# One program instead of three in a hybrid decoder step, values stationary, and the softmax divided before its transposes

## The chip, the cores and the metric

The kernel runs on one core of a Trainium2 chip. The metric is the device time of one execution in microseconds (us). Names of engines: TensorE (PE, its weight loads PEld), VectorE (DVE), ScalarE (ACT), GpSimd (POOL), and SyncE (SP), which here issues every DMA.

## The reference, cut to what matters

One layer of a decoder over 2048 prompt tokens and 32 sample tokens (8 sequences of 4 steps), model width 1024, everything in float32:

```
proj = x @ w_in                        # 22 column tiles of 128 and 8 gate columns
A: mLSTM, 4 heads of 128, chunkwise: scores, decay, a state C (128x128) and n per head
B: attention in a window of 128, 8 query heads on 2 key heads of 64, with a sink per head:
   mx = max(max(s), snk);  p = exp(s - mx)
   p / (sum(p) + exp(snk - mx))        # then @ v
x = LayerNorm(alpha * x + concat(A, B) @ w_out)
x = LayerNorm(alpha * x + (silu(x @ w1) * (x @ w3)) @ w2)
```

Outputs are both token groups' activations, the states, and the last 128 keys and values.

## The kernel before, in words

**Products.** Tokens are split into five groups of 416 columns (`TG`). A matrix is taken in slabs of 8 tiles of 128x128 (512 KB). To keep float32 accuracy, ScalarE rounds a slab to `whi`, GpSimd takes the rest `wlo = raw - whi`, and TensorE makes three products per tile, hi*hi, hi*lo and lo*hi, so a slab is 24 matmuls of 416 columns (`product`, L258). x is split in the same way, in quarters (`round_x`, `split_x`) when a visit of a token group begins. `raw` and `wlo` have four buffers, `whi` three: the load of slab n+3 waits for slab n-1, its rounding for slab n.

**Three programs.** `mixers` runs slabs 0 to 133 (110 of the projection, then those of the output product), `tail` slabs 134 to 149, `layer` the five groups' FFN, 60 slabs each. Each is a Block of its own, so all engines meet at its end.

**The order.** Every engine walks the same slabs n; tables written out by hand say after which slab what is done. `BASES` gives the slab at which a chunk of 128 tokens begins, `PIECES` its six pieces: TURN (transposes of k and v, first window scores, mLSTM scores), MIX (transposes of the first two exponentials, mLSTM outputs, state products), WIN (other window scores, first values), TURN2 (transposes of the other exponentials), VALUES (other values, transposes of the mLSTM output), OUT (`turn_out`: transposes of the attention's output `ow`). Most chunks have the offsets (0, 2, 3, 5, 6, 7), five have (0, 1, 2, 3, 4, 5). `LOAD_X_AT` and `SPLIT_AT` place the loads and splits of x, `ROWS_AT` the loads of a chunk's gate rows, broadcast over the partitions, `GATES_AT` the gate tables' chain.

**The attention in a chunk.** `window_max` adds the bias to the scores and takes the maximum; `window_exp` on ScalarE writes the exponentials to `pw` and their sums to `psums`; `turn_window` transposes them; `copy_turned` copies them to `ptw`. `window_values` has `ptw` stationary and 64 columns of v moving: 16 matmuls a chunk. In `valued`, VectorE divides by sums and sink into `ow`, four transposes turn it, and ScalarE copies it to `mix`.

**The tail.** The samples' inputs are loaded at slab 134 (`load_sample`), their scores, heads, transposes and outputs follow after slabs 135 to 138. Their mix goes to DRAM, and the last visit of the output product (slab 142 on) reads it with the prompt's part. The first LayerNorm of the first group stands at slabs 138 to 142 (`NORM`), eight state updates at 143 to 146 (`UPDATES`), the first FFN slabs' loads and rounding at 143 and after.

**The layer.** While a group's FFN runs, two LayerNorms are under way, one step per slab: SUM 0, MEAN 1, CENTRE 2, SQUARE 3, SUM_SQ 4, VARIANCE and ROOT 5, SCALE 6. The last group's second LayerNorm stands at the end, alone.

Of the kernel before, what the change touches and what calls it, by code (L numbers as in the profile page):

```python
# [48 lines left out]
X_AT = LIMIT - 2 * KD * TG * 4  # L49
assert AHEAD_AT % 32 == 0  # L50
# [20 lines left out]
class Store:  # L71


    def __init__(self, nc, ctx, at, end=LIMIT):
        self.nc, self.ctx, self.at, self.end = nc, ctx, at, end
# [9 lines left out]

    def ps(self, name, shape):
        return self.ctx.enter_context(self.nc.psum_tensor(name, shape, F32))
# [5 lines left out]
def load_gates(sp, io, t):  # L93
# [5 lines left out]
    for i, (n, bias) in enumerate((("gi", "b_ig"), ("gf", "b_fg"))):  # L99
# [18 lines left out]
CUT = PROJ + 3 * KD  # L118
# [9 lines left out]
LOAD_X_AT = (None, None, 3, 6, 9, 22, 44, 66, 88, 110, 118, 126, 141)  # L128
SPLIT_AT = (None, (0, 0, 1, 1), (3, 4, 4, 4), (6, 7, 7, 7), (9, 10, 10, 10), (26, 27, 32, 33), (47, 48, 54, 55), (69, 70, 76, 77),
            (97, 98, 103, 104), (112, 113, 115, 116), (120, 121, 123, 124), (128, 129, 131, 132), (141, 141, 141, 141))  # L130
# [3 lines left out]
PIECES = tuple(tuple(b + o for o in (FIVE if c in (1, 9, 10, 11, 14) else SEVEN)) for c, b in enumerate(BASES))  # L134
# [4 lines left out]
ROWS_AT = (21,) + tuple(b + 1 for b in BASES[:-1])  # L139
# [38 lines left out]
class Stream:  # L178


    def __init__(self, nc, ctx, io, m):
# [3 lines left out]
        self.raw = Store(nc, ctx, m.at).sb("raw", [P, 4, KD, P])  # L185
# [3 lines left out]
        for b, a in enumerate((Store(nc, ctx, X_AT), m)):  # L189
            self.xh.append(a.sb(f"xh{b}", [P, KD, TG], F32R))  # L190
            self.xraw.append(Store(nc, ctx, a.at).sb(f"xraw{b}", [P, KD, TG]))
            self.xl.append(a.sb(f"xl{b}", [P, KD, TG], F32R))
        self.ring_at = m.at

        self.stage = [Store(nc, ctx, m.at + (i * RING + FREE) * 4).sb(f"stage{i}", [P, TG]) for i in range(STAGES)]
# [15 lines left out]
    def load_x(self, sp, v, q):  # L211

        last = {2: gate_tile(1), 3: gate_tile(2), 4: gate_tile(3)}.get(v)
        if 5 <= v <= MIXED + 1:
            last = slab_tile((v - 4) * NPROJ - 1)
        if v > MIXED + 1:
            last = slab_tile(PROJ + (v - MIXED - 1) * KD - 1)
        if last is not None:
            sp.wait_ge(self.acc_full, last + 1)
        ks, (g, b) = slice(q * XQ, q * XQ + XQ), VISITS[v]  # L220
        src = self.io["xT"][g, :, ks] if v < MIXED else self.io["mixT"][ks, :, g * TG:g * TG + TG].rearrange("t p n -> p t n")
        sp.dma_start(self.xraw[b][:, ks], src).then_inc(self.x_in[v % 2][q], 16)
# [69 lines left out]
def mixers(nc, io, ctx, keep, outs, s_inp, stream):  # L292
# [5 lines left out]
    with ExitStack() as ctx:  # L298
        m = Store(nc, ctx, x.ring_at, X_AT)
        ring = m.sb("ring", [P, NPROJ, RING])  # L300

        xs = m.sb("xs_b", [P, H, 2, C])
        bias = m.sb("bias", [P, 8, SPAN])
        state, nlast, mix, mix_out, kv_out, st_out = (outs[n] for n in ("state", "nlast", "mix", "mix_out", "kv_out", "st_out"))
        causal = m.sb("causal", [P, C])
        ones = m.sb("ones", [P, 1])
        sinks = m.sb("sinks", [P, 8])
        gml = m.sb("gml", [P, H])
        vaug = m.sb("vaug", [P, H, P + 1])
        vs = m.sb("vs", [P, 2, P])  # L310
        pw = m.sb("pw", [P, 2, 2, SPAN])
        shared = m.at

        t = Store(nc, ctx, shared, X_AT)
        g = {n: t.sb(n, s) for n, s in (
            ("gi", [R, C]), ("gf", [R, C]), ("gi_s", [H, NS]), ("gf_s", [H, NS]),
            ("small", [R, 4]), ("small_s", [H, 4]), ("m0_sb", [H, DB]))}
        g["loaded"] = t.sem("g_loaded")
        gi, gf, gis, gfs, small, small_s, m0, g_loaded = (
            g[n] for n in ("gi", "gf", "gi_s", "gf_s", "small", "small_s", "m0_sb", "loaded"))  # L320
        tile = lambda n: (t.sb(n, [R, C]), t.sb(n + "_s", [H, NS]))
        b, b_s = tile("b")
        run, runs = tile("run")
        u, us = tile("u")
        em, ems = tile("em")
        own = t.sb("own", [R, C])
        gx, gxs = t.sb("xs", [R, 2, C]), t.sb("xss", [H, 2, NS])
        ones_r = t.sb("ones_r", [R, C])
        m_last = t.sb("m_last", [H, DB])
        m_end = t.sb("m_end", [1, H])  # L330
        ends = t.sb("ends", [1, 2, H, NC])
        after = t.sb("after", [1, H, NC])
        before = t.sb("before", [1, H, NC])
        inherited = t.sb("inherited", [R, 1])

        early = Store(nc, ctx, x.ring_at + EARLY * RING * 4, x.ring_at + NPROJ * RING * 4)
        anti = early.sb("anti", [P, P])
        hank = early.sb("hank", [P, 8, SPAN])
        srow = early.sb("srow", [32, 132])
        repl = early.sb("repl", [32, P])  # L340
        srow_all = early.sb("srow_all", [P, 132])
        smask = early.sb("smask", [P, 2, NS])
        onehot = early.sb("onehot", [32, HJ])
        relb = early.sb("relb", [32, 8])
        outside = early.sb("outside", [8, HJ])
        ext = early.sb("ext", [8, HJ])
        graw = early.sb("graw", [P, KD, 8])
        ghi = early.sb("ghi", [P, KD, P], F32R)
        glo = early.sb("glo", [P, KD, P], F32R)
        grow = early.sb("grow", [8, 2, TG])  # L350

        w = Store(nc, ctx, shared, X_AT)
        decay = w.sb("decay", [P, H, C])
        qs = w.sb("qs", [P, H, C])

        hn = Store(nc, ctx, w.at).sb("hn", [P, H, P])
        prob = w.sb("prob", [P, H, C])
        ow = Store(nc, ctx, w.at).sb("ow", [P, 4, P])
        kw = w.sb("kw", [P, H, P])
        den = w.sb("den", [P, H])  # L360
        ucol = w.sb("ucol", [P, 2, 2, H])
        rec = w.sb("rec", [P, H])
        ssq = w.sb("ssq", [P, H])
        root = w.sb("root", [P, H])
        gate = w.sb("gate", [P, H, C])
        sq8 = w.sb("sq8", [P, J, C])
        nmx = w.sb("nmx", [P, 8])
        mx = w.sb("mx", [P, 8])
        psums = w.sb("psums", [P, 2, 8])
        snk = w.sb("snk", [P, 8])  # L370
        ptw = w.sb("ptw", [P, 2, 4, W])

        acc = [m.ps(f"acc{i}", [P, 512]) for i in range(2)]
        w01 = m.ps("w01", [P, 2, 512])
        ce = m.ps("ce", [P, 2, 512])
        kd, fb = m.ps("kd", [P, 512]), m.ps("fb", [P, 512])
        heads_out = ce[:, :, 0:258].rearrange("p b (h e) -> p b h e", e=P + 1)
# [31 lines left out]
        def place(c):  # L409
            return slice(c * C % RING, c * C % RING + C)  # L410
# [1486 lines left out]
```

## Time and profile before

| | us |
|---|---|
| median of 3 runs (lowest, highest) | 2575.45 (2573.36, 2578.94) |
| the profiled execution | 2576.87 |
| its span, first to last instruction | 2575.1 |
| TensorE busy | 2493.3 |
| GpSimd busy | 1287.1 |
| ScalarE busy | 937.3 |
| VectorE busy | 927.6 |

The profile is of one execution. Its span begins with the first instruction, and all times in the rows below count from there; the execution took 1.8 us more than the span.

### The profile page before, as it was taken

The numbers are of one execution on the slowest core, as the hardware profiler recorded it, in microseconds if no ns is written. First come the engines' busy times: TensorE is split into PE (matmuls) and PEld (weight loads), VectorE is DVE, ScalarE is ACT, GpSimd is POOL, SyncE is SP. The second block draws the span as 40 slices with busy tenths as digits, with TensorE's granted clock in tenths as the row PEclk, the third lists the DMA queues.
The fourth block names the chain that finished last, engine by engine and source line by source line (L and its number), as shares of the span: only waits on it lengthen the run. The fifth ranks groups of instructions, "written<-read, shape, count | busy, mean of one in ns | idle before, by whom it ended". The sixth has DMA issues, their size and how long they took to land.

```text
span 2575.1 us, 33629 instructions
## 1 busy us (share of the span) xinstructions
PE 2493.3 (97%) x13771; PEld 2427.3 (94%) x13771; DVE 927.6 (36%) x1535; ACT 937.3 (36%) x1415; POOL 1287.1 (50%) x544
## 2 busy tenths in 40 slices
PE   8989999999999988999999999999999999999997
PEld 7979999999999877899999999999999999999996
DVE  4345454444546444111424213421335114251104
ACT  3324444444455423222334224332244223342222
POOL 4444544445444434455545565555554555555552
PEclk9999999999999988999999999999999999999998
DMA  5443534434365663434334343344333443334331
GB/s 185 152 118 97 143 99 136 105 99 142 97 183 177 200 216 116 128 119 143 124 106 135 119 155 113 105 136 146 125 114 99 144 145 122 108 120 132 124 117 68
DMA packets 142480, 335.50 MB, mean 130 GB/s; under 512 B 14734, under 2 KB 79846, under 8 KB 141670
## 3 DMA queue, kind: packets, MB, share of 16 engines
q1 hardware_dynamic: 142326, 333.34, 41.4%
q8 instruction: 110, 1.80, 0.3%
q14 instruction: 44, 0.36, 0.0%
HBM read 305.05 MB, written 29.26 MB: 130 GB/s over the span
## 4 chain that ended last, share of the span: by engine, by line
PE 57%; DVE 2%; ACT 0%; issue 0%; ACTq 0%; DVEq 0%
PE l_acc L1670 19%; PE l_acc L1668 19%; PE l_acc L1669 19%; DVE l_total L1128 1%; DVE hl L1704 0%; PE var L1144 0%; PE mean L1140 0%; ACT nxt L1651 0%; DVE nxt L1763 0%; DVE part L1718 0%; DVE var L1765 0%; DVE hbuf L1700 0%; DVE nxt L1713 0%; ACT x_squares L1646 0%; DVE hh L1702 0%; DVE l_total L1718 0%
## 5 line engine op out<-in xcount | busy, mean ns | idle before, releaser
L1605 POOL TENSOR_TENSOR l_wlo<-l_raw,l_whi 128x1024 fp32r<-128x1024 f32 (+1 forms) x297 | 823.7, 2773 | 693.6 <-ACT l_whi L1614 693.6
L1614 ACT ACTIVATE l_whi<-l_raw 128x1024 fp32r<-128x1024 f32 (+1 forms) x297 | 340.8, 1148 | 1031.2 <-PE l_acc L1670 992.8
L253 POOL TENSOR_TENSOR wlo<-raw,whi 128x1024 fp32r<-128x1024 f32 x150 | 364.7, 2432 | 543.0 <-ACT whi L247 542.8
L1668 PE MATMUL l_acc<-xh,l_whi 128*128 128x416 f32 x1760 | 620.0, 352 | 7.9 <-PEq L1190 7.9
L1670 PE MATMUL l_acc<-xh,l_wlo 128*128 128x416 f32 x1760 | 621.9, 353 | 0.0
L1669 PE MATMUL l_acc<-xl,l_whi 128*128 128x416 f32 x1760 | 615.1, 350 | 0.0
L266 PE MATMUL acc<-xh,whi 128*128 128x416 f32 x1072 | 385.4, 359 | 0.0
L268 PE MATMUL acc<-xh,wlo 128*128 128x416 f32 x1072 | 378.1, 353 | 0.0
L267 PE MATMUL acc<-xl,whi 128*128 128x416 f32 x1072 | 375.5, 350 | 0.0
L1668 PEld LDWEIGHTS l_acc<-xh,l_whi 128*128 128x128 f32 x1760 | 331.0, 188 | 11.3 <-issue 8.8
L1669 PEld LDWEIGHTS l_acc<-xl,l_whi 128*128 128x128 f32 x1760 | 331.2, 188 | 6.7 <-issue 1.3
L1670 PEld LDWEIGHTS l_acc<-xh,l_wlo 128*128 128x128 f32 x1760 | 330.6, 188 | 2.0
L1700 DVE TENSOR_TENSOR hbuf<-silu,l_acc 128x416 f32<-128x416 f32 x110 | 64.6, 588 | 732.7 <-PE l_acc L1670 732.7
L247 ACT ACTIVATE whi<-raw 128x1024 fp32r<-128x1024 f32 x150 | 158.4, 1056 | 466.5 <-PE acc L268 269.4
L1668 PE MATMUL l_acc<-hh,l_whi 128*128 128x416 f32 x880 | 312.1, 355 | 0.0
L1669 PE MATMUL l_acc<-hl,l_whi 128*128 128x416 f32 x880 | 309.4, 352 | 0.0
L1670 PE MATMUL l_acc<-hh,l_wlo 128*128 128x416 f32 x880 | 308.6, 351 | 0.0
L267 PEld LDWEIGHTS acc<-xl,whi 128*128 128x128 f32 x1072 | 202.2, 189 | 2.4
L268 PEld LDWEIGHTS acc<-xh,wlo 128*128 128x128 f32 x1072 | 201.6, 188 | 2.3
L266 PEld LDWEIGHTS acc<-xh,whi 128*128 128x128 f32 x1072 | 202.2, 189 | 1.4 <-POOL wlo L253 0.3
L1668 PEld LDWEIGHTS l_acc<-hh,l_whi 128*128 128x128 f32 x880 | 167.0, 190 | 2.5 <-issue 1.4
L1670 PEld LDWEIGHTS l_acc<-hh,l_wlo 128*128 128x128 f32 x880 | 165.2, 188 | 1.7
(333 smaller groups left out, 2567.6 us busy)
## 6 DMA issues: line engine op xcount, KB each, us to landing
l_raw<-in_wB SPq DMA_DIRECT2D x220, 512.0 KB, 3.6
raw<-in_wA SPq DMA_DIRECT2D x110, 512.0 KB, 3.7
l_raw<-in_w SPq DMA_DIRECT2D x80, 704.0 KB, 4.0
raw<-in_wB SPq DMA_DIRECT2D x40, 512.0 KB, 4.1
xraw<-in_xT SPq DMA_DIRECT2D x32, 416.0 KB, 5.6
xraw<-mixT SPq DMA_DIRECT2D x20, 416.0 KB, 6.5
stage<-in_xT SPq DMA_DIRECT2D x40, 208.0 KB, 4.2
pre<-stage SPq DMA_DIRECT2D x40, 208.0 KB, 4.1
```

Of the source, the lines that this page charges most:

```text
L247: self.nc.scalar.activation(self.whi[:, n % 3], self.raw[:, n % 4], ACT.Copy).then_inc(self.hi_done, 1)
L253: self.nc.gpsimd.tensor_tensor(self.wlo[:, n % 4], self.raw[:, n % 4], self.whi[:, n % 3].bitcast(F32), ALU.subtract).then_inc(self.lo_don ...
L266: pe.matmul(bank[:, 0:TG], hi[:, a], self.xh[x][:, a], start=(a == 0), stop=False)
L267: pe.matmul(bank[:, 0:TG], hi[:, a], self.xl[x][:, a], start=False, stop=False)
L268: last = pe.matmul(bank[:, 0:TG], lo[:, a], self.xh[x][:, a], start=False, stop=(a == KD - 1))
L1128: self.nc.vector.tensor_reduce(self.total[:], self.over_tiles(sq), AX.X, ALU.add).then_inc(self.sq_summed, 1)
L1605: nc.gpsimd.tensor_tensor(wlo[:, n % 4, 0:k], raw[:, n % 4, 0:k], whi[:, n % 3, 0:k].bitcast(F32), ALU.subtract).then_inc(S["lo_done"], 1)
L1614: nc.scalar.activation(whi[:, n % 3, 0:k], raw[:, n % 4, 0:k], ACT.Copy).then_inc(S["hi_done"], 1)
L1668: pe.matmul(bank, whi[:, n % 3, c], hx[:, a], start=(a == 0), stop=False)
L1669: pe.matmul(bank, whi[:, n % 3, c], lx[:, a], start=False, stop=False)
L1670: last = pe.matmul(bank, wlo[:, n % 4, c], hx[:, a], start=False, stop=(a == total - 1))
L1700: nc.vector.tensor_tensor(hbuf[:], silu[:, j % 2], acc[:, t % BANKS, 0:TG], ALU.mult).then_inc(S["evac"], 2)
```

## The change

All three parts become functions of one Block. The banks of the accumulators are shared by name, and where the end of a Block kept memory apart, counters are awaited (`Chunks.done`, `ring_read`, `updated`).

In a chunk, ScalarE scales the exponentials by one over (sum and sink's exponential) before they are transposed, per head (`divide`); v is stationary and `ptw` moves, 256 columns at a time, so that the result has the mix's layout. `turn_out`, `ow` and its multiplication are gone.

The samples' inputs are loaded from slab 130, and their mix is written straight into the last visit's x. Slab tables are changed.

```diff
-CUT = PROJ + 3 * KD
+CUT = PROJ + 3 * KD - 1
-LOAD_X_AT = (None, None, 3, 6, 9, 22, 44, 66, 88, 110, 118, 126, 141)
-SPLIT_AT = (None, (0, 0, 1, 1), ..., (26, 27, 32, 33), ..., (141, 141, 141, 141))
-SEVEN, FIVE = (0, 2, 3, 5, 6, 7), (0, 1, 2, 3, 4, 5)
-BASES = (24, 31, 37, 44, 51, 58, 66, 73, 80, 88, 94, 100, 106, 113, 120, 126)
-ROWS_AT = (21,) + tuple(b + 1 for b in BASES[:-1])
+LOAD_X_AT = (None, None, 3, 6, 9, 30, 44, 66, 88, 110, 118, 126, 135)
+SPLIT_AT = (None, (-1, -1, 0, 0), ..., (34, 35, 40, 41), ..., (139, 139, 140, 140))
+BASES = (24, 31, 37, 44, 51, 58, 66, 73, 80, 88, 94, 100, 106, 113, 119, 126)
+PIECES = tuple(tuple(b + o for o in (0, 2, 3, 5, 6, 6)) for b in BASES)
+SAMPLE_AT = BASES[-1] + 4
+ROWS_AT = (22,) + tuple(b + 1 for b in BASES[:-1])
-        GATES_AT = 15
+    GATES_AT = 14
...
@@ sync of the mixers
+        x.load(sp, 3)
             for n in range(CUT):
+            if n:
                 x.load(sp, n + 3)
-                if n == GATES_AT + 5:
+            if n == GATES_AT + 6:
                     sp.wait_ge(ga, SCALES)
+            if n == SAMPLE_AT:
+                chunks.ring_read(sp)
+                load_sample(sp, io, sample)
@@ tensor
-                wait(pe, "p_exp", c, r + 1)
+            wait(pe, "p_normed", c, r + 1)
-            def window_values(c, r):
-                wait(pe, "pt_copied", c, r + 1)
-                for gr in range(2):
-                    for half in range(2):
-                        last = pe.matmul(fb[:, r * P + gr * 64:r * P + gr * 64 + 64], ptw[:, r % 2, 2 * gr + half],
-                                         vs[:, s if half else 1 - s, gr * 64:gr * 64 + 64], ...
+        def window_values(c, pair):
+            wait(pe, "pt_copied", c, 2 * pair + 2)
+            for half in range(2):
+                for gr in range(2):
+                    last = pe.matmul(fb[64 * gr:64 * gr + 64, pair * 2 * W:pair * 2 * W + 2 * W], vs[:, s if half else 1 - s, gr * 64:gr * 64 + 64],
+                                     ptw[:, :, 2 * gr + half], start=(half == 0), stop=(half == 1))
-            def turn_out(c):
-                wait(pe, "ow_ready", c)
-                for r in range(J):
-                    last = pe.transpose(ce[:, 1, r * C:r * C + C], ow[:, r], ident[:])
-                last.then_inc(S["o_turned"], 1)
@@ scalar
+        def sink_exp(c, pair):
+            wait(act, "snk_arg", c, pair + 1)
+            a = slice(4 * pair, 4 * pair + 4)
+            nc.scalar.activation(snk[:, a], snk[:, a], ACT.Exp).then_inc(S["snk_exp"], 1)
+        def divide(c, pair):
+            wait(act, "rs_ready", c, pair + 1)
+            for r in (2 * pair, 2 * pair + 1):
+                for gr in range(2):
+                    last = nc.scalar.activation(pw[:, r % 2, gr], pw[:, r % 2, gr], ACT.Identity, scale=snk[:, 2 * r + gr:2 * r + gr + 1])
+                last.then_inc(S["p_normed"], 1)
@@ vector: sums after the exponentials, no ow
+        def sums(v, c, pair):
+            wait(dve, "snk_exp", c, pair + 1)
+            wait(dve, "p_exp", c, 2 * pair + 2)
+            v(nc.vector.tensor_tensor(snk[:, a], snk[:, a], psums[:, s, a], ALU.add))
+            nc.vector.reciprocal(snk[:, a], snk[:, a]).then_inc(S["rs_ready"], 1)
@@ tail
-    FIRST, SCORES, HEADS, TURNED, OUT, NORM, UPDATES = (CUT + i for i in (0, 1, 2, 3, 4, 4, 9))
+    FIRST, SCORES, HEADS, TURNED, OUT, UPDATES = (CUT + i for i in (0, 1, 2, 3, 4, 6))
+    HIGH_AT, FFN_AT = LAST + 2, LAST + 2
+    mix = x.xraw[VISITS[-1][1]][:, :, SEQ - (NG - 1) * TG:TG]
+    norm_at = {"sum": CUT + 1, "mean": CUT + 2, "centre": CUT + 3, "square": CUT + 4, "sum_sq": CUT + 5, "variance": CUT + 7, "scale": CUT + 8, "gain": CUT + 9}
-                if n == OUT + 1:
-                    sp.wait_ge(sig["mixed"], 3)
-                    sp.dma_start(io["mixT"][:, :, SEQ:NT].rearrange("t p n -> p t n"), mix[:]).then_inc(S["mix_out"], 16)
+            if n == LOAD_X_AT[-1]:
                     sp.wait_ge(outs["mix_out"], 16 * NC)
-                    sp.wait_ge(S["mix_out"], 16)
@@ layer
-    SUM, MEAN, CENTRE, SQUARE, SUM_SQ, VARIANCE, ROOT, SCALE, GAIN, HIGH, LOW = 0, 1, 2, 3, 4, 5, 5, 6, 7, 9, 10
+    SUM, MEAN, CENTRE, SQUARE, SUM_SQ, VARIANCE, ROOT, SCALE, GAIN, HIGH, LOW = 0, 1, 2, 3, 4, 6, 6, 7, 8, 10, 11
@@ layer, the last LayerNorm: four adds for two reduces, ScalarE squares and copies the mean, GpSimd centres tiles 4 to 7
+        for k in range(4, KD):
+            nc.gpsimd.tensor_tensor(x[:, k], x[:, k], silu[:, 1], ALU.subtract).then_inc(centred_rest, 1)
-            sum_part(part, 0, 0, 4)
-            sum_part(norm.total, 1, 4, 7)
+        add_squares(x_squares[:, 0:2], slice(0, 2), slice(2, 4), 1)
+        add_squares(part[:], 0, 1, 2)
+        add_squares(x_squares[:, 4], 4, 5, 3)
+        add_squares(norm.total[:], 4, 6, 4)
```

## Rows read from the trace of the kernel before

**Rows 1.** The page: busy time of each engine.
```profile
PE 2493.3 (97%) x13771; PEld 2427.3 (94%) x13771; DVE 927.6 (36%) x1535; ACT 937.3 (36%) x1415; POOL 1287.1 (50%) x544
```

**Rows 2.** Stretches of TensorE: length, busy (instructions), granted clock, DMA share, GB/s.
```profile
161.09:176.99 15.90, 6.54 (x31) 0.68 0.48 184
886.33:897.12 10.79, 6.64 (x23) 0.68 0.64 174
904.48:914.28 9.80, 5.20 (x45) 0.65 1.11 374
935.50:948.37 12.87, 12.87 (x53) 0.60 0.36 99
959.65:979.04 19.39, 5.72 (x15) 0.56 0.18 56
992.79:1003.07 10.28, 7.45 (x28) 0.67 0.33 96
1028.05:1040.54 12.49, 4.62 (x14) 0.73 0.61 188
886.33:1036.27 149.94, 116.82 (x619) 0.83 0.55 174
1200.00:1250.00 50.00, 50.00 (x266) 1.00 0.39 126
```

**Rows 3.** TensorE's waits: waiter, releaser, us in total, times, longest.
```profile
PE var L1144 <- DVE l_total L1128: 5.3, 4, 1.3
...
PE w L590 <- ACT pw L719: 3.0, 3, 1.3
...
PE acc L266 <- DVE ring L869: 2.2, 1, 2.2
```

**Rows 4.** Timeline of TensorE in chunk 2's WIN: start, us, instruction.
```profile
278.54 1.14 PE L577 MATMUL w<-ring,sq 64*128 64x256 f32 x8
279.61 2.00 PE L599 MATMUL fb<-vs,ptw 128*128 128x64 f32 x16
281.42 0.44 PE L266 MATMUL acc<-xh,whi 128*128 128x416 f32 x1
```

**Rows 5.** Timeline of TensorE: bias tables (512 columns), samples' window scores.
```profile
54.06 1.98 PE L677 MATMUL w<-hank,anti 128*128 128x512 f32 x4
55.88 1.88 PE L677 MATMUL ce<-hank,anti 128*128 128x512 f32 x4
...
909.43 0.68 PE L1326 MATMUL s_wi<-s_kc,s_qb 128*32 128x128 f32 x8 [4.60 <-DMA s_state<-in_state_C]
...
909.98 0.67 PE L1326 MATMUL s_wi<-s_kc,s_qb 128*32 128x128 f32 x8
```

**Rows 6.** Timeline of chunk 12: ScalarE's last exponential, then TensorE's MIX.
```profile
715.88 0.50 ACT L719 ACTIVATE pw<-pw,nmx 128x256 f32<-128x256 f32 x1
716.28 0.19 ACT L719 ACTIVATION_READ_ACCUMULATOR pw<-pw,nmx 128x1 f32 x1
...
719.15 0.60 PE L590 MATMUL w<-ident,pw 128*128 128x128 f32 x4
```

**Rows 7.** Timeline of SP's issues, before chunk 0 and in the tail.
```profile
146.68 1.13 SPq L489 DMA_DIRECT2D xsT<-xs  x2
...
151.23 7.22 SPq L222 DMA_DIRECT2D xraw<-in_xT  x4
...
897.63 6.31 SPq L1094 DMA_DIRECT2D s_state<-in_state_C  x4
```

**Rows 8.** Timeline of VectorE in the tail.
```profile
943.72 6.06 DVE L1120 TENSOR_REDUCE t_total<-nxt 128x416 f32<-128x3328 f32 x1
...
974.27 3.82 DVE L280 TENSOR_TENSOR xl<-xraw,xh 128x832 fp32r<-128x832 f32 x4
```

**Rows 9.** The chain that ended last, its end: start, us, what.
```profile
2550.39 3.19 DVE part L1718
2553.59 1.50 DVE l_total L1718
...
2560.71 3.59 DVE nxt L1763 x2
```

More of the change, by code:

```diff
@@ new lines, in mixers @@
+    m = Store(nc, x.ring_at, X_AT)
+    ring = m.sb("ring", [P, NPROJ, RING])
+    xs = m.sb("xs_b", [P, H, 2, C])
+    bias = m.sb("bias", [P, 8, SPAN])
+    state, nlast, mix, mix_out, kv_out, st_out = (outs[n] for n in ("state", "nlast", "mix", "mix_out", "kv_out", "st_out"))
+    causal = m.sb("causal", [P, C])
+    ones = m.sb("ones", [P, 1])
+    sinks = m.sb("sinks", [P, 8])
+    gml = m.sb("gml", [P, H])
+    vaug = m.sb("vaug", [P, H, P + 1])
+    vs = m.sb("vs", [P, 2, P])
+    pw = m.sb("pw", [P, 2, 2, SPAN])
@@ new lines, in mixers @@
+    shared = m.at
+    t = Store(nc, shared, X_AT)
+    g = {n: t.sb(n, s) for n, s in (
+        ("gi", [R, C]), ("gf", [R, C]), ("gi_s", [H, NS]), ("gf_s", [H, NS]),
+        ("small", [R, 4]), ("small_s", [H, 4]), ("m0_sb", [H, DB]))}
+    g["loaded"] = t.sem("g_loaded")
+    gi, gf, gis, gfs, small, small_s, m0, g_loaded = (
+        g[n] for n in ("gi", "gf", "gi_s", "gf_s", "small", "small_s", "m0_sb", "loaded"))
+    tile = lambda n: (t.sb(n, [R, C]), t.sb(n + "_s", [H, NS]))
+    b, b_s = tile("b")
@@ new lines, in mixers @@
+    run, runs = tile("run")
+    u, us = tile("u")
+    em, ems = tile("em")
+    own = t.sb("own", [R, C])
+    gx, gxs = t.sb("xs", [R, 2, C]), t.sb("xss", [H, 2, NS])
+    ones_r = t.sb("ones_r", [R, C])
+    m_last = t.sb("m_last", [H, DB])
+    m_end = t.sb("m_end", [1, H])
+    ends = t.sb("ends", [1, 2, H, NC])
+    after = t.sb("after", [1, H, NC])
+    before = t.sb("before", [1, H, NC])
+    inherited = t.sb("inherited", [R, 1])
+    early = Store(nc, x.ring_at + EARLY * RING * 4, x.ring_at + NPROJ * RING * 4)
@@ L1179, in layer_inputs, with tail @@
     }
[L1182 removed]
+def tail(nc, io, keep, s_inp, outs, stream, chunks, taken, ahead, norm, ps):
     cols, ident, sbias = keep["cols"], keep["ident"], keep["sbias"]
@@ L1519, in layer @@
-def layer(nc, io, keep, stream, ahead):
+    LAST = PROJ + 4 * KD - 1
+    FIRST, SCORES, HEADS, TURNED, OUT, UPDATES = (CUT + i for i in (0, 1, 2, 3, 4, 6))
+    HIGH_AT, FFN_AT = LAST + 2, LAST + 2
+    m = taken["rest"]
+    inp, (xs, state, n0, kc, vc, causal, sinkcol, gml) = s_inp, (
+        taken[n] for n in ("xs", "state", "n0", "kc", "vc", "causal", "sinkcol", "gml"))
+    expo = m.sb("s_expo", [NS, H, NS])
+    decay = m.sb("s_decay", [NS, H, NS])
+    prob = m.sb("s_prob", [NS, H, NS])
```

2460 lines of the change are left out of this document (1225 added, 1235 removed).

## The prediction, made before the changed kernel ran

> **What bounds the kernel now.** I read the page first. TensorE is busy 97% of the span [rows 1], so a microsecond is won only by giving it less to do, by closing its gaps, or by not letting its clock fall. Second, the stretches: in an undisturbed one the granted clock is 1.00 and 266 products of 416 columns start in 50 us, 0.188 us each [rows 2]. With that price any other stretch can be audited: its length less the work in it is what was lost. Third, the waits of TensorE [rows 3] and the order of time in one chunk say whose fault a loss is.
>
> The audit. From 886.33, where the first program's last piece begins, to 1036.27, where the layer begins, are 149.9 us [rows 2]. The work is 16 slabs of 24 products (72.2 us) and the samples' pieces (I add their pieces in the timeline to 28.3 us): 100.5 us. So 49 us are lost, one by one [rows 2]: 10.8 us for 0.4 + 3.5 of work at the first program's end (6.9 lost); 9.8 us for 3.3 of work before the samples' scores (6.5); 19.4 us for 2.8 before the last visit (16.6); 10.3 for 5.7 at the first state updates (4.6); 12.5 for 2.6 at the second program's end (9.9); and some 4 at half clock around the samples' last matmuls. Each loss has two parts: the gap, and a restart in which the clock stands at 0.5 for some us: the mean clock of these stretches is 0.56 to 0.73. Elsewhere: 15.9 us at chunk 0 for 8 products and its TURN, 4.0 of work (11.9 lost) [rows 2]; 2.2 us on a ring copy in the fourth slab; 3.0 us on the exponentials in three chunks that have one slab between TURN and MIX; and four waits at the variance, 5.3 us in all [rows 3].
>
> **The change, part by part.**
>
> *Values stationary.* Now each chunk makes 16 matmuls of 64 columns on full arrays, in two passes each: the 16 records from 279.61 to the next slab at 281.42 are 0.11 us each [rows 4]: 1.73 us and the way back to full slabs. VALUES holds the other 16 and four transposes of 0.09. New: 8 matmuls of 256 columns, 16 passes, each half writing 64 of the 128 output partitions. The nearest rows for 256 columns are the scores: 8 passes from 278.54 to 279.61, 1.07 us [rows 4]. At half the price of 512 columns (4 records from 54.06 to 55.88, 0.455 us each [rows 5]) they would take 0.23 each and 1.8 us one after another, so the two row halves run side by side. I read the 1.07 us as four steps of 0.215 and 0.2 for two changes of the array's shape. Column parts of the array run side by side too: the samples' scores write 32 partitions each, and the first 8 records of 128 columns, with 8 of 32 behind them, are through in 0.55 us (909.43 to 909.98 [rows 5]), where one after another at half clock the 8 alone would take over 1.7. I therefore take 4 x 0.215 = 0.86 for each half chunk instead of 1.73, and 0.1 for each of three more changes of the array's shape. WIN: 2.87 becomes 2.03; VALUES: 2.09 becomes 1.42; the four transposes of `turn_out` (0.36) go. That is 1.87 a chunk, 29.9 us in 16. Bounds: passes one after another give 16 x 0.215 = 3.44 against 3.46, so the part is worth only 5.8 - 4.8 = 1 us; no cost for the shape changes gives 34.7.
>
> The Trainium skill (TensorEngine Tiling, "Key Properties") has the rule that speaks against this: changing the tiling mode drains the engine, while tiles of one mode run independently. The trace agrees with both halves, at about 0.1 us a change. If a drain cost twice that, the sum would be 4.8 us worse.
>
> *The division moves to ScalarE.* Eight scalings of 128x256 a chunk. The exponentials of that shape start 0.41 us apart without the accumulator read [rows 6], so 3.3 us a chunk on an engine that is busy 36% [rows 1]. What hides it is the distance between TURN and MIX, now always two slabs. In the latest chunk (12) the second exponentials end at 716.37 [rows 6]; the sink's exponential and two small VectorE operations add 0.7, four scalings 1.7: 718.8, and MIX starts at 719.15. Margin 0.3 us; chunk 11 is as close, chunk 14, held up by a split on VectorE, may wait, and the rest have 0.7 to 2 by the same reading. The next slab's rounding moves from 716.9 to 719, with its rest on GpSimd 2.4 us later still, two slabs ahead of need. On VectorE the `sums` stand before the value copy, `prob` and `kw`, all needed only at MIX. Cost on the path: 2 us in all. The 3.0 us of waits in one-slab chunks go.
>
> *Gate tables and the load queue.* The 9.4 us gap before chunk 0 is SP's: it stood until 146.68 for the tables, then queued rows and four x loads of 416 KB before the slabs [rows 7]. The tables now run one slab earlier, rows one later, the x load eight later: all 11.9 us go. The wait of 1.9 us for the samples' chain before the tables' transposes keeps its distance and stays. In the start, two splits precede the loop and slab 3's load no longer stands behind the bias table: 2.2 us go [rows 3].
>
> *One program.* The barriers go. The chunks' counters are awaited after slab 133; the last piece is in slab 132, so nothing is late: 6.9 us. At the other end the first FFN slabs are rounded earlier, nothing waits: 9.9 us.
>
> *Samples' inputs.* Eleven loads are issued at slab 130 instead of 134; TensorE's gap and its restart, 6.5 us [rows 2], go. But SP stood 6.3 us at the last four alone before [rows 7], some 12 at all eleven, and the slab load behind them is now as late as that: issue, 4 us landing, rounding and rest end about when slab 134 is due. I charge 2 us.
>
> *The last visit.* Before, its four quarters were loaded only after the samples' mix had gone through DRAM, and their splits stood behind mean, variance and scaling on VectorE: a reduce of 6.1 us, one like it, and then the splits at 974.27 [rows 8]. Now the prompt's part is loaded at 135, the samples' part is written in place, and sum, centre and squares come earlier. By my placing of VectorE's work the splits end some 5 us before slab 142: 16.6 us go. The updates move to slabs 139 to 142 between splits and scaling (3.6 + 2.7 us on VectorE), where update b waits for b-2: I expect three waits of 1 to 3 us, 4 of the 4.6 us remain in another place. Gain 0.6.
>
> *Variance one slab later.* VectorE's 6.2 us reduce no longer ends after TensorE's slab: four times (1.3 gap + 0.5 slow restart), 7.2 us.
>
> *The end.* The sums of squares, 3.19 + 1.50 us [rows 9], become four adds of 2.9 together; they end 1.8 us earlier, at the last slab's end. ScalarE reads the mean while TensorE makes the last variance product, level with the two VectorE operations it replaces. Half of the centring (1.8 of 3.59 us [rows 9]) leaves the chain for GpSimd, which has 3 us to spare before the fifth tile is due; the root with its table load (2 us) fits under the other half. I take 3.5 us.
>
> **Sum.** 29.9 - 2 + 3.0 + 11.9 + 2.2 + 6.9 + 9.9 + 6.5 - 2 + 16.6 + 0.6 + 7.2 + 3.5 = 94.2 us. The profiled execution took 2576.9 us (span 2575.1): 2482.7. The median of the three runs is 1.4 lower: 2481 us.
>
> **Rivals.**
> - *Passes of the two column halves run one after another* (chance 0.10). For: they read the same partitions of the moving tile in two streams of 256 columns, which no row shows at full clock. Against: [rows 5]. 29 us less gained: 2510.
> - *The tail keeps a stall* (0.16): SP's late slab load, or VectorE late with splits or updates so that slab 142 waits, each with a restart at half clock as in [rows 2]. For: reduces of 6 us in an engine with strict order, margins of a few us. Against: each of these operations has a slab or more between its due time and its need by my placing. 16 of the 38.5 us won there would be given back, three such restarts: 2497.
> - *MIX waits for the division* (0.10): margin 0.3 us in chunk 12. If sums or scalings take 1.5 us more than I say, all chunks wait, 16 x 1.3 = 20 us: 2501.
> - *The clock falls in the new pieces* (0.02), the one that ends slower. The samples' matmuls on narrow parts of the array begin at 935.5 at full clock, and yet the stretch to 948.37 has a mean of 0.60, with TensorE busy all of it [rows 2]. If both column-tiled pieces of each chunk did that, 32 times, it decides from 94/32 = 2.9 us each; that stretch lost about 5, which would give 2576 + 66 = 2642. Against: the new pieces last 0.86 us, not 7.5, with wide streams, and the row-tiled scores beside them run at a clock of 1.00.
> - *More than forecast* (0.05): updates and slab 134 without a wait, no restart after the samples: about 2470.
> - The forecast, 0.57; its own range is 2470 to 2492.
>
> The range reaches to the second and third rival and leaves out the first and fourth (0.12): 2466 to 2504. A difference under 0.2%, 5 us, can't be told from none here. Only the clock rival is slower, and equality would need several rivals at once: faster 0.97, same 0.01, slower 0.02.
>
> **What would show it.** In the profile after: 8 fb matmuls a chunk whose records come in pairs about 0.2 us apart (else the first rival); WIN near 2.0 us; a clock of 1.00 in every stretch from 200 to 850; no wait of TensorE on `pw`; no gap before chunk 0; no gap on PEq at the two former boundaries; the way from slab 133's end to the layer near 108 us instead of 150; no wait at `var`. Wrong it would be if TensorE waited in new places for `pw`, `xl`, `s_state` or `wlo`.

## The result and the profile after

The changed kernel takes 2489.06 us (median of 4 runs, 2486.23 to 2490.38), the kernel before beside it 2577.19 (4 runs, 2573.36 to 2581.67). The ratio is 0.9656 with a 95% interval of 0.9637 to 0.9675: 88.1 us faster. The forecast was 2481, 94 us won, with a range of 2470 to 2492 of its own and of 2466 to 2504 with the rivals. The profiled span went from 2575.1 to 2486.4, so 88.7 us can be followed in the two traces.

The page after (compare [rows 1]): ScalarE has 54 us more work, TensorE 46 us less, and TensorE is still the bound.
```profile
PE 2447.4 (98%) x13451; PEld 2366.3 (95%) x13451; DVE 912.0 (37%) x1566; ACT 991.3 (40%) x1561; POOL 1304.0 (52%) x548
```

TensorE's waits after (compare [rows 3]). Nothing waits for `pw`, nothing in the layer for the variance, and no gap is put down to TensorE's own queue. The first two lines are new: `ptw` are the turned exponentials, copied by ScalarE, and `hn` the normalized heads of the mLSTM, made by VectorE; TensorE had waited for neither in the kernel before.
```profile
PE fb L620 <- ACT ptw L751: 6.8, 1, 6.8
PE kd L672 <- DVE hn L977: 5.8, 8, 2.5
...
PE ce L1331 <- DVE s_state L1542: 2.7, 2, 1.4
```

Stretches of TensorE after, with the columns of [rows 2] and the other engines' busy time between: chunk 0 from the tables on; all chunks from 200 us to the last MIX; chunk 15's second transposes and values with slab 133; from slab 133's end to the layer.
```profile
149.00:170.46 21.46, 21.46 (x127) 20.84 (x126) 9.30 (x22) 10.40 (x24) 11.77 (x6) 1.00 0.55 121
200.00:810.44 610.44, 607.21 (x3694) 565.33 (x3693) 306.64 (x849) 360.01 (x827) 303.06 (x154) 1.00 0.48 139
...
835.20:853.34 18.14, 8.83 (x39) 7.09 (x38) 7.47 (x8) 5.14 (x7) 6.97 (x7) 0.72 0.55 165
853.34:961.26 107.92, 105.25 (x615) 98.42 (x614) 62.13 (x100) 38.13 (x50) 53.13 (x25) 0.95 0.59 193
```
The way to the layer is 107.9 us where it was 149.9. But the stretch before it, 18.14 us with 8.83 of work at a mean clock of 0.72, is a new hole.

I cut the span at landmarks that both traces have and set the gain of each part beside the terms of the prediction:

| part | forecast | measured |
|---|---|---|
| start to the bias tables (53.64, now 49.72) | 2.2 | 3.9 |
| from there to MIX of chunk 0 (185.31, now 170.46) | 11.9 | 10.9 |
| to MIX of chunk 15 (853.94, now 810.44) | 15 x 1.87 + 3.0 - 2 = 29.05 | 28.65 |
| to slab 133's end and on to the layer (1036.27, now 961.26) | 38.5 + 1.87 = 40.4 | 31.5: 42.0 won behind slab 133, 10.5 lost before it |
| to the last mean (2545.83, now 2462.56) | 7.2 | 8.3 |
| the end | 3.5 | 5.4 |
| sum | 94.25 | 88.7 |

Five of six parts lie within 2 us of their forecast; nearly all that is missing was lost at one place, chunk 15.

**The pieces.** WIN of chunk 12 after (compare [rows 4]):
```profile
692.34 1.14 PE L597 MATMUL w<-ring,sq 64*128 64x256 f32 x8
693.40 1.08 PE L620 MATMUL fb<-ptw,vs 128*64 128x256 f32 x8
694.42 0.46 PE L268 MATMUL acc<-xh,whi 128*128 128x416 f32 x1
```
2.08 us, forecast 2.03, before 2.87. VALUES takes 1.43 (forecast 1.42) where nothing waits. The eight records come in pairs 0.216 us apart, 7 ns within a pair. That they run side by side can be read against matmuls of the same type over the whole array, a few us on in the same trace:
```profile
685.02 0.39 PE L653 MATMUL ce<-vaug,prob 128*128 128x129 f32 x2
685.24 0.39 PE L654 MATMUL ce<-state,qs 128*128 128x129 f32 x2
```
Two records of 129 columns take 0.22 us, so two of 256 would take 0.44 and eight 1.75; here eight are through in 0.87 and some 0.15 for the change of shape. The records don't say which half of the columns they belong to; that the two of a pair belong to different halves is my reading (see experiment 9).

**Chunk 15.** SyncE's issues, then ScalarE, VectorE and TensorE, around 825 to 847 us. In square brackets is the idle time before an instruction and what ended it:
```profile
825.70 6.09 SPq L1132 DMA_DIRECT2D s_state<-in_state_C  x4
831.83 1.66 SPq L209 DMA_DIRECT2D raw<-in_wB  x1
...
839.41 1.06 ACT L249 ACTIVATE whi<-raw 128x1024 fp32r<-128x1024 f32 x1 [8.85 <-DMA raw<-in_wB]
840.38 0.88 ACT L243 ACTIVATE xh<-xraw 128x832 fp32r<-128x832 f32 x1
841.16 1.06 ACT L751 ACTIVATE ptw<-w 128x512 f32<-128x512 f32 x2
...
841.29 2.49 DVE L282 TENSOR_TENSOR xl<-xraw,xh 128x832 fp32r<-128x832 f32 x1 [10.60 <-ACT xh L243]
843.70 0.16 DVE L975 RECIPROCAL root<-root 128x4 f32<-128x4 f32 x1
843.90 2.10 DVE L976 TENSOR_TENSOR rec<-rec,root 128x4 f32<-128x4 f32 x1
...
842.28 1.98 PE L620 MATMUL fb<-ptw,vs 128*64 128x256 f32 x8 [6.79 <-ACT ptw L751]
846.78 1.11 PE L672 MATMUL kd<-ident,hn 128*128 128x128 f32 x4 [2.52 <-DVE hn L977]
```
Read it from the top. SyncE stands 6.1 us at the last four of the samples' loads; only then does it ask for the weights of slab 134. They land at 839.4, and ScalarE, which takes its work in strict order, has stood 8.85 us idle for them. Behind that rounding are queued the rounding of a quarter of x and the copies of chunk 15's turned exponentials, both of them ready long before. TensorE waits 6.8 us for the copy. VectorE waited 10.6 us for the quarter, splits it ahead of the normalized heads, and TensorE waits 2.5 us more. The first products behind it then start 0.35 us apart instead of 0.19, at a granted clock of 0.5.

**The end** (compare [rows 9]), from the chain that ended last: the centring is down from 3.59 us to 1.79 in the chain. Of the sums of squares, 3.19 + 1.50 us before, one add of 1.04 us is left in it.
```profile
2473.83 1.79 DVE nxt L1812
2475.63 2.68 DVE w L1814
```
The eight products of mean and variance in front of it, before and after, with the columns of the stretches above:
```profile
2555.13:2559.95 4.82, 4.75 (x8) 2.10 (x8) 2.08 (x4) 1.83 (x2) 0.00 (x0) 0.65 0.00 0
2470.07:2473.20 3.13, 3.06 (x8) 1.43 (x8) 1.17 (x2) 1.28 (x3) 0.00 (x0) 1.00 0.00 0
```
Before, TensorE had waited 2.1 us for the sums and then made these products at a mean clock of 0.65. Now it waits 0.3 us and makes them at 1.00, in 1.7 us less.

### The profile page after: what moved, and what is told of

Its sections match the earlier page's. It is cut to its first block, busy times and chain, and to the rows that moved or that the text cites. A ratio compares the mean times of both kernels' runs of the same rounds, so it can differ in the third digit from the quotient of the medians.

```text
span 2486.4 us, 33138 instructions
## 1 busy us (share of the span) xinstructions
PE 2447.4 (98%) x13451; PEld 2366.3 (95%) x13451; DVE 912.0 (37%) x1566; ACT 991.3 (40%) x1561; POOL 1304.0 (52%) x548
## 3 DMA queue, kind: packets, MB, share of 16 engines
q8 instruction: 107, 1.75, 0.3%
## 4 chain that ended last, share of the span: by engine, by line
PE 91%; DVE 4%; ACT 3%; issue 1%; DMA 1%; SPq 1%; ACTq 0%; DVEq 0%
PE acc L1719 10%; PE acc L1717 10%; PE acc L1718 10%; PE acc L268 8%; PE acc L270 8%; PE acc L269 8%; PE kd L1719 5%; PE fb L1719 5%; PE kd L1717 5%; PE fb L1717 5%; PE kd L1718 5%; PE fb L1718 5%; DVE xl L282 1%; PE w L610 1%; PE w L597 1%
## 5 line engine op out<-in xcount | busy, mean ns | idle before, releaser
L1717 PE MATMUL acc<-xh,l_whi 128*128 128x416 f32 x880 | 310.9, 353 | 0.0
L1719 PE MATMUL acc<-xh,l_wlo 128*128 128x416 f32 x880 | 310.6, 353 | 0.0
L1718 PE MATMUL acc<-xl,l_whi 128*128 128x416 f32 x880 | 307.2, 349 | 0.0
L1718 PEld LDWEIGHTS acc<-xl,l_whi 128*128 128x128 f32 x880 | 165.3, 188 | 4.0 <-issue 1.3
L1717 PEld LDWEIGHTS acc<-xh,l_whi 128*128 128x128 f32 x880 | 165.2, 188 | 2.2 <-issue 1.3
L1719 PEld LDWEIGHTS acc<-xh,l_wlo 128*128 128x128 f32 x880 | 165.0, 188 | 1.0
L1717 PE MATMUL acc<-hh,l_whi 128*128 128x416 f32 x440 | 156.2, 355 | 0.0
L1719 PE MATMUL fb<-xh,l_wlo 128*128 128x416 f32 x440 | 155.3, 353 | 0.0
L1719 PE MATMUL kd<-xh,l_wlo 128*128 128x416 f32 x440 | 155.3, 353 | 0.0
L1718 PE MATMUL acc<-hl,l_whi 128*128 128x416 f32 x440 | 154.7, 352 | 0.0
```

The lines of the kernel that those rows point to most:

```text
L1717: pe.matmul(bank, whi[:, n % 3, c], hx[:, a], start=(a == 0), stop=False)
L1718: pe.matmul(bank, whi[:, n % 3, c], lx[:, a], start=False, stop=False)
L1719: last = pe.matmul(bank, wlo[:, n % 4, c], hx[:, a], start=False, stop=(a == total - 1))
```

## The experiments

All are edits of the changed kernel. Times are medians; their differences are against its 2489.06.

**1. State loads later** (e1). The five loads of the samples' state leave `load_sample` for a function of their own, which takes the first and last of them to issue.
```diff
             if n == SAMPLE_AT:
                 load_sample(sp, io, sample)
+            if n == SAMPLE_AT + 1:
+                load_state(sp, io, sample, 0, 2)
+            if n == SAMPLE_AT + 2:
+                load_state(sp, io, sample, 2, 4)
...
             if n == CUT:
+                load_state(sp, io, taken, 4, 5)
```


> The five loads of the samples' state leave slab 130 of SyncE's order and go out at slabs 131 (two), 132 (two) and 133 (one). Theory A (the stall in chunk 15 is the load queue's: the weights of slab 134 are asked for behind eleven loads and land late, their rounding waits on ScalarE, and the copy of the turned exponentials and the quarter's rounding stand behind it): TensorE's waits of 6.8 and 2.5 us at VALUES of chunk 15 and the slow restart go, slab 133 ends near 843 us instead of 853.3, and the time is 9 to 10.5 us shorter, about 2479. Rival B (ScalarE is late there by its own work, the eight scalings that the change gave it): the waits stay, 2489. Rival C (the state now lands late for the samples' heads in slab 135): TensorE waits there on the state for some us, and a part of the gain is lost, 2482 to 2486.

Measured: 2478.94 us (2476.91 to 2481.75), ratio to before 0.9619, interval 0.9606 to 0.9633; 10.1 us faster. The wait for `ptw` is gone, of the eight waits for `hn` the longest is 0.8 us, and slab 133 ends at 842.04 instead of 853.34. SyncE asks for the weights of slab 134 at 825.22, where it had asked at 831.83, and their rounding, which had started at 839.41 after 8.85 us of idle time, starts here:
```profile
825.22 0.33 SPq L209 DMA_DIRECT2D raw<-in_wB  x1
...
830.97 1.06 ACT L249 ACTIVATE whi<-raw 128x1024 fp32r<-128x1024 f32 x1 [0.75 <-DMA raw<-in_wB]
```
So 6.6 of the 8.4 us are the later asking. The rest is a slower landing, which took 7.6 us behind the four loads and 5.8 us here.
Theory A held in place and size. The state is not late for the heads.

**2. Order in two engines** (e2). ScalarE copies before it rounds, VectorE normalizes before it splits, in every chunk; the loads are those of the changed kernel.
```diff
-            x.round_slab(act, n + 3)
             for c in at_piece(n, TURN2):
                 copy_turned(c, 2)
                 copy_turned(c, 3)
+            x.round_slab(act, n + 3)
...
             x.add(dve, acc, n)
+            for c in at_piece(n, TURN2):
+                normed(v, c)
             for k in range(1, len(VISITS)):
```


> Loads as in the changed kernel; only the order in two engines is changed, in every chunk: ScalarE copies the turned exponentials before it rounds a slab, VectorE normalizes before it splits a quarter of x. Theory A: the late weights are themselves early enough for slab 134 (they land near 839 us, rounding and rest end near 844, and the slab is due after 845), only what is queued behind their rounding hurt. So the stall goes just as with later loads, 9 us, and the seven waits of 0.46 us on the normalized heads go too, 3 us: about 2477. Rival (the late weights themselves hold TensorE): a wait on the rest of slab 134 of 3 to 8 us takes the place of the old one, 2480 to 2487. Rival B (ScalarE's own work is what is late): no gain but the 3 us, 2486.

Measured: 2485.45 us (2483.55 to 2487.52), 3.6 faster, in a range that overlaps the changed kernel's; the reading rests on the trace. Both waits in chunk 15 go, and another takes their place, which neither theory named:
```profile
843.92 2.66 DVE L282 TENSOR_TENSOR xl<-xraw,xh 128x832 fp32r<-128x832 f32 x1
846.50 0.68 DVE L986 SCALAR_TENSOR_TENSOR mixed<-kd,gate 128x512 f32<-128x512 f32 x1
...
847.28 0.58 PE L1342 MATMUL kd<-ident,s_inp 128*32 128x128 f32 x2 [5.44 <-DVE mixed L986]
```
The quarters' rounding still stands behind the late weights, the splits behind it, and the mix of chunk 15 behind the splits. The samples' transposes (L1342) write the bank that this mix still reads. So a late load that nobody needs yet reached TensorE by a second way. The order decides which waiter is hit; the cure is the load. The waits of 0.46 us for `hn` did not go either (seven, 3.2 us in all): my reading that a split in front causes them was wrong (see the last section).

**3. Three blocks again** (e3).
```diff
+        for sync, gpsimd, tensor, scalar, vector in parts:
+            with nc.Block() as block:
+                block.sync(sync)
+                ...
```


> The changed kernel in three blocks again, with the barrier after slab 132 and the one after the last slab of the first product. By the prediction's two terms it loses 6.9 us at the first and 9.9 us at the second, 16.8 in all: 2506, with gaps of TensorE's queue of 4 to 6 us at both places and a slow restart behind each. Rival: at the first boundary the stall of chunk 15 covers part of it, and the rounding of the first slabs behind the second boundary is done before it, so that only 5 to 10 us are lost: 2494 to 2499.

Measured: 2503.38 us (2502.45 to 2508.14), 14.3 slower. Two gaps on TensorE's queue are back:
```profile
PE kd L1717 <- PEq L1857: 7.9, 1, 7.9
...
PE acc L268 <- PEq L1857: 3.8, 1, 3.8
```
From slab 133's end to the layer it takes 117.6 us (856.21 to 973.84) against 107.9: 9.7 for the second barrier, forecast 9.9. From the second transposes of chunk 15 to slab 133's end it takes 28.2 us against 23.4: 4.8 for the first, forecast 6.9. The stall of chunk 15 is in both.

**4. Window values twice** (e4).
```diff
-            for half in range(2):
+            for half in (0, 1, 0, 1):
                 for gr in range(2):
                     last = pe.matmul(fb[64 * gr:64 * gr + 64, ...
```


> The eight matmuls of 256 columns that make a chunk's window values are issued twice, into the same place, so the output stays. If the two halves of the array's columns run side by side, four of them add 0.87 us, and 32 groups add 28 us: 2517. If their passes run one after another, four take 1.7 to 1.8 us and 32 groups add 56 us: 2545. If the clock fell in them, more than that, with a granted clock under 0.98 in the chunks.

Measured: 2509.91 us (2507.88 to 2510.70), 20.9 slower, with a granted clock of 0.993, as in the changed kernel (0.992 to 0.994). The price of four matmuls is read from WIN of chunk 12:
```profile
708.53 1.95 PE L620 MATMUL fb<-ptw,vs 128*64 128x256 f32 x16
710.41 0.46 PE L268 MATMUL acc<-xh,whi 128*128 128x416 f32 x1
```
1.88 us to the next slab against 1.02, so 0.86 for four: side by side, 27.5 us in 32 groups. The time rose less because a longer VALUES covers the waits for `hn` (5.8 us in the changed kernel, 0.8 here) and 0.9 of the stall in chunk 15.

**5 and 6. The two moves before chunk 0, each undone** (e5: the x load; e6: the tables).
```diff
-LOAD_X_AT = (None, None, 3, 6, 9, 30, 44, ...     SPLIT_AT: (34, 35, 40, 41)
+LOAD_X_AT = (None, None, 3, 6, 9, 22, 44, ...     SPLIT_AT: (26, 27, 32, 33)
...
-    GATES_AT = 14
+    GATES_AT = 15
```


> One part undone: the fifth visit's x is loaded at slab 22 again (after: 30) and split at 26, 27, 32 and 33; the gate tables and the rows keep their new places. Theory A (the gap of 9.4 us before chunk 0 was SyncE's queue, rows and four x loads ahead of the slabs, released late by the tables): the tables are done earlier now, so the queue starts a slab earlier, but the four x loads stand ahead of the rows and of two slabs again; TensorE waits 3 to 7 us before chunk 0 with a restart, 2493 to 2497. Rival B (the tables' place alone removed the gap): chunk 0 starts as before, 2489.

> The other part undone: the gate tables run at slabs 15 to 21 again (after: 14 to 20), the rows of chunk 0 at 22 and the x load at 30 as in the changed kernel. Theory A: SyncE stands about one slab longer for the tables, but only rows and slabs are behind it; TensorE loses 0 to 3 us before chunk 0, 2489 to 2492. Rival B (the tables' place is what removed the gap): the wait on the tables or on the rows returns before chunk 0, 5 to 12 us, 2494 to 2501.

Measured: 2494.52 us (2492.99 to 2497.94) with the x load back, 5.5 slower; 2488.68 (two runs, 2485.84 and 2491.52) with the tables back, no difference. MIX of chunk 0 is 5.4 us later in the first (175.87) and not later in the second (169.80). The x load's mark is the same pattern as in chunk 15, a rounding that waits for its weights with the next chunk's scaled queries behind it:
```profile
161.05 1.06 ACT L249 ACTIVATE whi<-raw 128x1024 fp32r<-128x1024 f32 x1 [10.71 <-DMA raw<-in_wA]
162.01 0.61 ACT L757 ACTIVATE sq<-ring 128x512 f32<-128x512 f32 x1
...
162.77 1.23 PE L601 MATMUL w<-ring,sq 64*128 64x128 f32 x8 [4.52 <-ACT sq L757]
```
The x load explains half of the 11 us won there. Alone, the tables' slab is worth nothing; that both together bring back the rest was not tried.

**7. Variance one slab earlier** (e7).
```diff
-    SUM, MEAN, CENTRE, SQUARE, SUM_SQ, VARIANCE, ROOT, ... = 0, 1, 2, 3, 4, 6, 6, ...
+    SUM, MEAN, CENTRE, SQUARE, SUM_SQ, VARIANCE, ROOT, ... = 0, 1, 2, 3, 4, 5, 5, ...
```


> The layer's variance product and the root stand one slab earlier again (step 5 instead of 6; scale, gain and the rest keep their new steps). By the prediction's term TensorE waits 1.3 us at the variance and restarts slowly, 7.2 us in four places: 2496. Rival: the waits return (5 us in all), but the restart at half clock costs little, because the gaps are short: 2494.

Measured: 2495.11 us (2491.51 to 2498.92), 6.05 slower, between the two. The waits of [rows 3] are back to the tenth:
```profile
PE w L1182 <- DVE total L1166: 5.3, 4, 1.3
```
From 1000 to 2400 us TensorE starts 34 fewer matmuls, 34 x 0.19 = 6.5 us. So 5.3 of waiting and about 1 of restarts.

**8 and 10. More work on ScalarE before the division**, of the first pairs of heads (e8) and of the second (e10, `pair == 1`).
```diff
             wait(act, "rs_ready", c, pair + 1)
+            if pair == 0:
+                for r in range(2):
+                    for gr in range(2):
+                        nc.scalar.activation(pw[:, r, gr], pw[:, r, gr], ACT.Copy).then_inc(S["copied"], 1)
+                wait(act, "copied", c, 4)
```


> Before it divides the first two pairs of heads, ScalarE copies each of the four tiles of 128x256 onto itself once more, so the division of the first half ends some 1.8 us later (four copies of 0.41 us and a drain); the result stays. The prediction gave chunk 12 a margin of 0.3 us before MIX, chunk 11 the same and the others 0.7 to 2. If those margins are right, TensorE waits for the exponentials before MIX in nearly every chunk, 0 to 1.5 us, 12 to 20 us in all: 2501 to 2509. If the margins are wider than I read, fewer than five chunks wait and the time is under 2494.

> The four extra copies on ScalarE now stand before the division of the second two pairs of heads (1.4 us), not of the first. In the profile after, that division ends 0.3 us before the second transposes in 8 of 16 chunks, 2.2 to 2.5 us before them in six, 0.9 before in one, and late in one. If the margin there is what the change stands on, nine chunks now wait 0.5 to 1.8 us each, 9 to 12 us in all: 2498 to 2501, and the next rounding of a slab is late too. Rival (ScalarE has room in front of that division as well, because what precedes it is a wait): 2489 to 2491.

Measured: 2488.95 us (2486.78 to 2492.76) before the first, nothing lost; 2501.61 (2500.87 to 2505.15) before the second, 12.5 slower. The copies delayed the division by 1.4 us in both. In the changed kernel, ScalarE's division of chunk 12 and TensorE's MIX, then its second division in chunk 1 and the transposes that take it:
```profile
679.53 1.71 ACT L742 ACTIVATE pw<-pw,snk 128x256 f32<-128x256 f32 x4
...
684.15 1.03 PE L610 MATMUL w<-ident,pw 128*128 128x128 f32 x8
...
229.30 1.28 ACT L791 ACT_TABLE_LOAD   x1
...
230.71 1.70 ACT L742 ACTIVATE pw<-pw,snk 128x256 f32<-128x256 f32 x4
...
232.70 1.03 PE L610 MATMUL w<-ident,pw 128*128 128x128 f32 x8
```
Before MIX chunk 12 has 684.15 - 681.24 = 2.9 us; the least of all chunks is 0.85 (chunk 13), and there the copies make the division end after the first transposes have begun, without a wait. Before the second transposes 8 of 16 chunks have 0.3 us, since the root with its table load stands in front of the second division. With the copies there:
```profile
PE kd L672 <- DVE hn L982: 11.3, 10, 2.5
...
PE w L610 <- ACT pw L747: 4.5, 18, 0.9
```
4.5 us wait for `pw`, and the waits for `hn` grow by 5.5: rounding and rest of the next slab come later too, and VectorE's normalizing with them.

**9. Column halves apart** (e9).
```diff
-            for half in range(2):
-                for gr in range(2):
+            for gr in range(2):
+                for half in range(2):
                     last = pe.matmul(fb[64 * gr:64 * gr + 64, ...
```


> Same eight matmuls a chunk, another order: both blocks of keys for one half of the array's columns, then both for the other, where the changed kernel alternates between the halves. Theory A (a matmul of one column half runs beside its neighbour in the queue only if that one uses the other half): of four matmuls only the middle two can overlap, so four take three steps of 0.43 us instead of two, 1.3 us instead of 0.87, and 32 groups cost 14 us more: 2503. If also the middle two don't overlap, 28 us more: 2517. Rival B (the order doesn't matter, what made the pieces short is the wider moving tile alone): 2489.

Measured: 2490.39 us (2487.06 to 2490.54), no difference that this can tell (ratio to before 0.9659, interval 0.9643 to 0.9675, against 0.9656). WIN of chunk 12:
```profile
692.93 1.09 PE L620 MATMUL fb<-ptw,vs 128*64 128x256 f32 x8
693.95 0.46 PE L268 MATMUL acc<-xh,whi 128*128 128x416 f32 x1
```
1.02 us again, its records again in pairs, 13 ns within a pair. Theory A falls: a half's matmul need not stand beside one of the other half in the program. But it is still two streams at once, since one after another they would take 1.75 us; so rival B's "order doesn't matter" holds and its "wider tile alone" does not.

One rival is left by this: that the two of a pair are the two passes of one matmul, and not one matmul of each half. No run makes a half's matmuls alone, which would settle it. Against it are two signs. The distance in a pair grows from 7 to 13 ns when the partner in the other half stands two matmuls further on instead of one. And the scores of [rows 4] have been in this order all along, both matmuls of one row half and then both of the other, each half with an increment of `win` at its end: of their eight records, in pairs 13 ns apart, the last two both carry that increment, so there a pair does hold one matmul of each half.

**11 and 12. Both cures, and the updates first** (e11 is e1 and e2 together; e12 also moves VectorE's state updates).
```diff
+            for b in range(DB):
+                if UPDATES + b // 2 == n:
+                    ...
             if n == norm_at["sum"]:
                 ...
             for q in range(4):
                 if SPLIT_AT[-1][q] == n:
                     x.split_x(dve, len(VISITS) - 1, q)
-            for b in range(DB):
-                if UPDATES + b // 2 == n:
-                    ...
```


> The later state loads and the other order in ScalarE and VectorE together. If the two effects add (10 us for the stall of chunk 15; 3.2 us for seven waits of 0.46 us and 0.8 us for the wait left in chunk 15), 2475; TensorE then waits on the normalized heads nowhere. Rival (copying first makes the rounding of a slab late elsewhere): 2478 to 2482.

> As the one before, and in the samples' part VectorE adds the updates of the state before it splits, scales or sums: the two waits of TensorE on the updated state (2.7 us, and their restart) should go, 2471 to 2472. Rival (the splits, now 3 to 5 us later, come too late for the last visit's first slab, and a wait on the low part of x takes their place): 2475 to 2480.

Measured: 2479.96 us (2478.35 to 2481.39) for both, 2473.67 (2470.22 to 2475.39) with the updates first. The order adds nothing to the later loads: the seven waits for `hn` stay, and in that profile TensorE waits 1.9 us in all for the first sum that its mean product takes. The updates' place brings 6.3 us, more than the 2.7 of its waits: two slow restarts between 903 and 925 us go with them (ten products each, 1.6 us over 0.188 us a product), and that other wait is down to 0.6:
```profile
PE kd L676 <- DVE hn L981: 3.2, 7, 0.5
...
PE w L1186 <- DVE total L1166: 0.6, 1, 0.6
```
The splits were not late for the last visit. This kernel beats both others: ratio to before 0.9597, interval 0.9583 to 0.9611, 103 us under it and 15 under the changed one.

## Why the prediction was right, and where its sum was off

- *Values stationary*: right. 0.79 us in WIN, 0.66 in VALUES, 0.36 for the turned output are 1.81 a chunk against 1.87. Experiment 4 fixes the price that the forecast had inferred from the samples' scores in [rows 5]: 0.86 us for four, forecast 0.86. The rivals of serial passes and of a falling clock did not come about; the clock was 1.00 from 200 to 810 us.
- *The division*: cost nothing at MIX, but the margin was misread. The 0.3 us of chunk 12 came from the exponentials in [rows 6], and those were late before for a reason that the change took away: ScalarE's rounding ahead of them had stood idle for its weights. This row of the kernel before says so; the prediction had not read it:
```profile
710.36 1.06 ACT L247 ACTIVATE whi<-raw 128x1024 fp32r<-128x1024 f32 x1 [6.05 <-DMA raw<-in_wA]
```
In the changed kernel the last exponential of chunk 12 ends 5.15 us before MIX, where it had ended 2.7 before. Experiment 8 shows that 1.4 us more is free there; experiment 10 that the thin margin is at the second transposes, which the prediction did not work out.
- *From chunk 0 to chunk 15*: 28.65 for 29.05 is in part luck. The 2 us charged for the division were not spent, and a wait of 1.6 us for VectorE's `state` in WIN of chunk 13 went, which nobody had counted; against that stand the seven waits for `hn`, 3.2 us, which the prediction didn't have. It took the 0.66 us in VALUES as won without asking what the transposes of `hn` behind it wait for; a VALUES that is longer again covers them (experiment 4).
- *One-slab chunks and wait on `pw`*: gone, as said.
- *Before chunk 0*: 10.9 of 11.9. The queue was the cause, as said; the x load carries 5.4 of it, the tables' slab alone nothing (experiments 5, 6).
- *Barriers*: the second 9.7 (forecast 9.9), the first 4.8 (forecast 6.9) with the stall beside it (experiment 3).
- *Samples' inputs, last visit, updates*: from slab 133's end 107.9 us, forecast near 108. Of three waits for updates that were expected two came, 1.3 and 1.4 us; with their restarts they cost about 5.9 where 4 was forecast, and experiment 12 gets 6.3 back.
- *"SP late slab load behind sample loads", 2 us*: the term that was mis-sized most, and the step that failed. The prediction asked when slab 134 needs its weights, and found them just in time; it did not ask what stands behind their rounding on ScalarE. That is the copy of chunk 15's exponentials and a quarter's rounding, and through the latter VectorE's split. It came in chunk 15 and not in the tail: the stretch from MIX to slab 133's end took 10.5 us more than before, where values stationary alone should have won 1.5, so the stall cost about 12. Moving the loads gives back 10.1 in the medians and 11.3 in the profiled executions (experiment 1). It is the mechanism of the second rival, at another place and with 12 instead of 16 us.
- *Variance*: forecast 7.2; 6.05 by experiment 7, with 8.3 between the layer's start and the last mean, so about 2 there have no experiment behind them.
- *Start and end*: 3.9 for 2.2 and 5.4 for 3.5, both more than forecast, neither taken apart by a run. At the end the trace shows the difference: 1.7 us are the eight products at full instead of half clock, a restart that the prediction had not priced there. At the start the ring wait of 2.2 us is gone as said. The rest lies within what the start varies by itself: in the profiles of experiments 1, 3, 5, 7 and 11, which leave the start as it is, the tables begin between 49.1 and 51.1 us.

The sum is 5.5 us off: 8.9 too much from chunk 15 to the layer, 3.6 too little at start and end, and small differences. That a range of 2470 to 2492 held is owed in part to terms that cancelled.

## What to carry to other kernels

When a load is delayed, don't ask only when its own consumer needs it; ask what is queued behind the instruction that waits for it, on each engine in turn. The same mark, a rounding with `<-DMA raw` and some us of idle time ahead of other work, stood in three places here (chunk 12 before, chunk 0 with the x load back, chunk 15 after). Ask the same of a piece that is made shorter: what stood ready behind it before may not be ready now. And a margin read from a trace belongs to that trace: look at what held up the engine there before counting on it or fearing it.

## What the runs showed of the hardware

VectorE's small operation in front of the normalized heads takes 0.16 to 2.10 us for four elements a partition. In 14 of the 16 chunks GpSimd's rounding rest is running when it starts, and it ends 0.01 to 0.02 us after that; in the other two (13 and 14) none is running, and it takes 0.16. VectorE and GpSimd in chunk 2, then in chunk 15, then chunk 5:
```profile
276.54 1.65 DVE L976 TENSOR_TENSOR rec<-rec,root 128x4 f32<-128x4 f32 x1
...
272.63 5.54 POOL L255 TENSOR_TENSOR wlo<-raw,whi 128x1024 fp32r<-128x1024 f32 x2 [8.32 <-ACT whi L249]
...
843.25 2.73 POOL L255 TENSOR_TENSOR wlo<-raw,whi 128x1024 fp32r<-128x1024 f32 x1 [0.35 <-ACT whi L249]
...
404.04 0.23 DVE L976 TENSOR_TENSOR rec<-rec,root 128x4 f32<-128x4 f32 x1
...
401.86 2.40 POOL L255 TENSOR_TENSOR wlo<-raw,whi 128x1024 fp32r<-128x1024 f32 x1 [6.39 <-ACT whi L249]
```
276.54 + 1.65 = 278.19 and 272.63 + 5.54 = 278.17; 843.90 + 2.10 = 846.00 and 843.25 + 2.73 = 845.98; 404.04 + 0.23 = 404.27 and 401.86 + 2.40 = 404.26. The reciprocal just before, with one input, takes 0.16 us in the middle of GpSimd's operation (843.70 in the lines on chunk 15). By these times the seven waits of 0.46 us are GpSimd's doing, which would be why no order on VectorE removed them and why experiment 10, in which GpSimd's rest came later, has eight of them, of 1.0 us each. The Trainium skill (SBUF — State Buffer, "Who interferes with whom") has the rule: a VectorE instruction with two inputs in SBUF contends with a GpSimd instruction that reads SBUF, the ports that the two share are an exclusive lock, and the order of issue decides who is blocked. The trace agrees to 0.02 us in these three places. No run here took GpSimd's operation away in a chunk that waits, so the cause of the waits is read from the times and not tested.

Unexpected too: matmuls that each write half of the output partitions run two at a time, 0.87 us for four, also where both of one half stand together in the program (experiment 9), and four loads of 512 KB can hold SyncE's queue for 6.1 us, while the same loads, issued one or two a slab, take 0.5 to 0.7 us each there.
